# Rows scaled before they are turned, and the last adaptation product moved behind the norm

## The reference, cut to what matters

```
x = x + 0.5 * swiglu(rms_norm(x, ffn1_norm[l]), gate, up, down)      # ffn1, 2816 wide
p = rms_norm(x, mix_norm[l]) @ w_in[l]                                # mixer: latent attention
x = x + concat(attn(p), conv(p)) @ w_out[l]                           #   and a 31-tap convolution
x = x + 0.5 * swiglu(rms_norm(x, ffn2_norm[l]), gate, up, down)      # ffn2
x = rms_norm(x, post_norm[l])
```

```
shift, scale, gate = split(silu(c) @ w_ada[l] + b_ada[l], 3)
h = rms(x, norm_w[l]) * (1 + scale) + shift
```

## Time and profile before

| | |
|---|---|
| median of 3 runs | 2732.62 us (2731.36 to 2739.61) |
| profiled execution, its own time | 2733.47 us |
| its span, first to last instruction | 2731.8 us |
| PE busy | 2438.5 us, 89% |
| PE weight loads busy | 2051.2 us, 75% |
| DVE busy | 1842.4 us, 67% |
| ACT busy | 1150.6 us, 42% |
| mean granted clock of PE | 0.938 |
| DMA moved | 298.41 MB, mean 109 GB/s |
| DMA of constants, latent weights, x | 1904, 2304 and 1024 KB |

### The profile page before, as it was taken

One profiled execution on the slowest core, in us unless ns is written; L12 is line 12 of the kernel. 1 busy time (PEld: TensorE's weight loads), 2 busy tenths in 40 slices (PEclk: granted clock), 3 DMA queues, 4 the chain that ended last, 5 costly groups with the idle time before them and its releaser, 6 DMA issues.

```text
span 2731.8 us, 38970 instructions
## 1 busy us (share of the span) xinstructions
PE 2438.5 (89%) x13968; PEld 2051.2 (75%) x13968; DVE 1842.4 (67%) x3484; ACT 1150.6 (42%) x1747; POOL 89.6 (3%) x140
## 2 busy tenths in 40 slices
PE   7998768997998868997999989999777899999978
PEld 6997458997997448996777777677456788888868
DVE  6775867787775776785455534456334699998884
ACT  4344334434344333334555513323223455555553
POOL 0000000000000000001122101001000000000000
PEclk9999969999999969998999989999888999999998
DMA  6554006555553005554344411111012222222212
GB/s 258 215 192 153 17 8 234 206 189 186 211 203 139 31 8 201 215 192 85 79 71 75 77 39 62 62 46 61 23 61 70 70 77 77 84 84 77 77 58 96
DMA packets 81319, 298.41 MB, mean 109 GB/s; under 512 B 9824, under 2 KB 10336, under 8 KB 80480
## 3 DMA queue, kind: packets, MB, share of 16 engines
q1 hardware_dynamic: 77760, 284.20, 29.4%
q0 software_dynamic: 2048, 4.20, 2.7%
q10 hardware_dynamic: 1440, 9.08, 0.9%
HBM read 296.39 MB, written 1.05 MB: 109 GB/s over the span
## 4 chain that ended last, share of the span: by engine, by line
PE 66%; DVE 24%; ACT 6%; issue 2%; DMA 1%; POOL 0%; DVEq 0%; SPq 0%; ACTq 0%; another core or an unknown queue 0%; POOLq 0%
PE ps L668 45%; PE ps L709 9%; DVE work L1900 3%; DVE wsplit L1761 3%; PE ps L1079 2%; DVE work L1816 1%; DVE work L2378 1%; DVE work L2348 1%; DVE work L2340 1%; PE ps L695 1%; DVE work L2399 1%; ACT wsplit L1241 1%; ACT work L1707 1%; PE ps L951 1%; PE ps L965 1%
## 5 line engine op out<-in xcount | busy, mean ns | idle before, releaser
L668 PE MATMUL ps<-hsplit,wsplit 128*128 128x256 f32 (+1 forms) x9072 | 1503.5, 325 | 32.5 <-DVE hsplit L2037 13.0
L668 PEld LDWEIGHTS ps<-hsplit,wsplit 128*128 128x128 f32 x9072 | 1313.0, 192 | 178.9 <-issue 22.9
L1241 ACT ACTIVATE wsplit<-ring 128x1024 fp32r<-128x1024 f32 x490 | 516.9, 1058 | 708.6 <-PE ps L668 499.0
L1761 DVE TENSOR_TENSOR wsplit<-ring,wsplit 128x1024 fp32r<-128x1024 f32 x490 | 600.8, 1230 | 299.0 <-ACT wsplit L1241 285.5
L709 PE MATMUL ps<-wsplit,fsplit 128*128 128x512 f32 x1056 | 261.5, 397 | 13.6 <-DVE wsplit L1761 8.7
L709 PEld LDWEIGHTS ps<-wsplit,fsplit 128*128 128x128 f32 x1056 | 195.1, 191 | 51.9 <-DVE wsplit L1761 9.6
L1816 DVE SCALAR_TENSOR_TENSOR work<-ring,cs,work 128x128 f32<-128x128 f32 x672 | 206.0, 348 | 9.0
L1316 ACT ACTIVATE work<-ps 128x256 f32<-128x256 f32 x88 | 33.7, 383 | 153.4 <-PE ps L668 153.4
L1900 DVE SCALAR_TENSOR_TENSOR work<-work,vec 128x256 f32<-128x256 f32 x240 | 97.6, 476 | 0.0
L1186 PE MATMUL ps<-work 128*128 128x128 f32 x512 | 71.1, 290 | 24.3 <-DVE work L2399 24.0
L1794 DVE TENSOR_TENSOR work<-ps,work 128x256 f32<-128x256 f32 x88 | 37.3, 424 | 77.0 <-ACT work L1316 76.6
(11 more groups left out here) (312 smaller groups left out, 2545.1 us busy)
## 6 DMA issues: line engine op xcount, KB each, us to landing
ring<-panels SPq DMA_DIRECT2D x538, 512.0 KB, 4.2
work<-latent_weights ACTq DMA_DIRECT2D x2, 2304.0 KB, 12.8
work<-rpb POOLq DMA_DIRECT2D x64, 64.0 KB, 6.7
cst<-constants ACTq DMA_DIRECT2D x1, 1904.0 KB, 9.6
work<-x SPq DMA_DIRECT2D x1, 1024.0 KB, 10.8
work<-post_rows ACTq DMA_DIRECT2D x2, 512.0 KB, 3.9
cT<-ctx ACTq DMA_DIRECT2D x1, 1024.0 KB, 6.6
out<-xT SPq DMA_DIRECT2D x1, 1024.0 KB, 3.9
```

The lines of the kernel that those rows point to most:

```text
L668: ins = mm(out_, w(a), x(b), start=start and n == 0, stop=stop and n == 2, **kw)
L1241: af(wsplit[:, split_slot(name, n), 0, :], ring[:, p % slots, :], ACT.Copy).then_inc(high_ready, 1)
L1761: tt(parts[:, 1, :], ring[:, p % slots, :], parts[:, 0, :].bitcast(fp32), ALU.subtract)\
```

## The change

- The identity scaled by the factors is gone. The rows are scaled instead, into `xs` (the place of `mix`): row tile 0 by DVE, row tile 1 by ACT (`scaled`), each in two instructions of 128 x 512. PE then turns the pieces with sixteen transposes, in the order half 0 of row tile 0, half 0 of row tile 1, and the same for half 1.
- `turned` reads a PSUM bank only when PE is through with it (`bank_full`). The turned tiles lie in seven banks, not eight, and bank 6 is left to the adaptation's sums.
- The twelfth adaptation product of each ffn section goes from the section's end to the next norm: tiles 0 to 5 between DVE's scaling and its `turned`, tiles 6 and 7 behind `turned`. PE's sum goes behind `turn`; the bias is added by `ada_out` behind that.
- In `post_factor` the Exp of `n_r1` is done once for both row tiles, behind the scaling.
- ACT issues only the identity's 128 columns of the constants and the two tables at the start, and the other constants and the latent weights behind its first factor and scaling. The sigmoid of the condition goes behind the first `turned`. DVE's `mixer`, PE's, and POOL wait for the rest of the constants.

```diff
-            def turn(q, src, banks):
-
-                for t in range(2):
-                    pe.wait_ge(row_stage, 4 * q + t + 3)
-                    for k in range(KD):
-                        ins = mm(turned_at(banks, k, t * 128, 128),
-                                 src[:, t, k * 128:(k + 1) * 128], diag_r[:, t, :], start=True, stop=True)
-                        if t == 1:
-                            ins.then_inc(t_done, 1)
+            def turn(q, banks):
+
+                for half in range(2):
+                    for t in range(2):
+                        pe.wait_ge(*((row_stage, 4 * q + 3 + half) if t == 0 else (rstd_ready, 3 * q + 2 + half)))
+                        for k in range(4 * half, 4 * half + 4):
+                            ins = nc.tensor.transpose(turned_at(banks, k, t * 128, 128), xs[:, t, k * 128:(k + 1) * 128],
+                                                      cst[:, K_ID:K_ID + 128])
+                            if t == 1:
+                                ins.then_inc(t_done, 1)
...
+            def ada_sum(l, f, n, i=0):
+
+                pe.wait_ge(ada_acc_ready, l * (2 * ADA_PER_FFN) + (i + (f * ADA_PER_FFN + n + 2)))
+                for v in range(2):
+                    last = mm(ps[:, 6, bass.ds(i * 2 + (2 * n + v), 1)], ada_acc[:, v, :], ones[:, 0:1],
+                              start=True, stop=True)
+                last.then_inc(ada_sum_done, 1)
...
                 down(3 * FT - 1, 1, fb + FT)
-                ada_sum(ADA_PER_FFN - 1)
...
-                turn(l * 3, xg, FFN_BANKS)
+                turn(l * 3, FFN_BANKS)
+                if l > 0:
+                    ada_sum(l - 1, 1, ADA_PER_FFN - 1)
                 ffn("ffn1", l, 0, l * 3)
                 pe.wait_ge(x_ready, l * 16 + 4)
-                turn(l * 3 + 1, xN, MIX_BANKS)
+                turn(l * 3 + 1, MIX_BANKS)
+                ada_sum(l, 0, ADA_PER_FFN - 1)
                 mixer(l)
...
-            turn(LAYERS * 3, xg, LAST_BANKS)
+            turn(LAYERS * 3, LAST_BANKS)
+            ada_sum(LAYERS - 1, 1, ADA_PER_FFN - 1)
             norm(0, sq_ctx)
...
+            def scaled(t, src):
+
+                for half in range(2):
+                    c = slice(half * 512, (half + 1) * 512)
+                    af(xs[:, t, c], src[:, t, c], ACT.Copy, scale=n_rr[:, t:t + 1]).then_inc(rstd_ready, 1)
...
-                for t in range(2):
-                    dve.wait_ge(rstd_ready, 2 * q + t + 1)
-                    ts(diag_r[:, t, :], cst[:, K_ID:K_ID + 128], n_rr[:, t:t + 1], None, ALU.mult).then_inc(row_stage, 1)
+                dve.wait_ge(rstd_ready, 3 * q + 1)
+                for half in range(2):
+                    c = slice(half * 512, (half + 1) * 512)
+                    ts(xs[:, 0, c], src[:, 0, c], n_rr[:, 0:1], None, ALU.mult).then_inc(row_stage, 1)
...
-                ada_products(SLOTS * (FT // 2) - 1, ADA_PER_FFN - 1)
...
                 V.restart()
-                row_factors(l * 3 + 1, 16 * l + 4, 2, 1)
+                row_factors(l * 3 + 1, 16 * l + 4, 2, 1, xN)
+                ada_last(l, 0, range(0, 6))
                 turned(l * 3 + 1, vec[:, V_MIX:V_MIX + 8], MIX_BANKS, "win", l)
+                ada_last(l, 0, range(6, KD))
+                ada_out(l, 0)
                 mixer(l)
...
-            act.dma_start(cst[:, :], consts_in).then_inc(const_loaded, 16)
+            act.dma_start(cst[:, 0:128], consts_in[:, 0:128]).then_inc(const_loaded, 16)
             act.dma_start(vec2[:, :], vec2_in).then_inc(const_loaded, 16)
             act.dma_start(vec[:, :].unsqueeze(1), vecs_in[0:1].rearrange("a p m -> p a m")).then_inc(const_loaded, 16)
-            act.dma_start(lat[:, :].unsqueeze(1), lat_in[0:1].rearrange("a p m -> p a m")).then_inc(lat_loaded, 16)
...
-            act.wait_ge(ada_in, 1)
-            sigmoid(cs[:, 0, :], cs[:, 0, :]).then_inc(ada_sig, 1)
             act.wait_ge(rows_loaded, 16)
             for b in range(4):
                 square(b, xg, 0).then_inc(sq_ready, 1)
-            factor(0)
+            factor(0, xg)
+            act.dma_start(cst[:, 128:NCONST], consts_in[:, 128:NCONST]).then_inc(const_loaded, 16)
+            act.dma_start(lat[:, :].unsqueeze(1), lat_in[0:1].rearrange("a p m -> p a m")).then_inc(lat_loaded, 16)
```

More of the change, by code:

```diff
@@ L341, in build @@
         a_qn = take(1)
-        gw = take(KD, 16)
+        gw = work[:, 20200:20328].rearrange("p (k g) -> p k g", k=KD)
         a_sq = sqf[:, 0:1024].rearrange("p (a t) -> p a t", a=2)
@@ L741, in ffn @@
                 down(4, 0, fb + 1, first=True)
-                ada_sum(0)
+                pe.wait_ge(ada_ready, 2 * l + f)
+                ada_sum(l, f, 0)
                 with pe.Fori(0, FT // 2 - 1) as i:
@@ L894, in _ @@
             pe.wait_ge(h_ready, H_FIRST + 8)
+            pe.wait_ge(ada_ready, 2 * LAYERS)
             for k in range(KD):
@@ L1270, in factor @@
                     A.need()
-                    af(n_rr[:, t:t + 1], n_l1[:, t:t + 1], ACT.Exp, scale=-0.5).then_inc(rstd_ready, 1)
+                    ins = af(n_rr[:, t:t + 1], n_l1[:, t:t + 1], ACT.Exp, scale=-0.5)
+                    if t == 0:
+                        ins.then_inc(rstd_ready, 1)
+                    else:
+                        A.did(ins)
+                        A.need()
+                scaled(1, src)
             def post_factor(q):
@@ L1281, in post_factor @@
                     A.did(af(n_h1[:, c], n_l1[:, c], ACT.Copy, scale=-0.5))
-                    A.did(af(n_r1[:, c], n_l1[:, c], ACT.Exp, scale=-0.5))
                     A.need()
@@ L1787, in normed, with ada_products @@
                     ts(xN[:, t, :], xg[:, t, :], n_r1[:, t:t + 1], None, ALU.mult).then_inc(x_normed, 1)
+            def ada_products(name, l, f, p, n, i=0, tiles=range(KD)):
+                w = ring[:, p % SLOTS, :].rearrange("p (k c) -> p k c", k=KD)
+                done = l * (2 * ADA_PER_FFN) + (i + (f * ADA_PER_FFN + n + 1))
+                if 0 in tiles:
+                    dve.wait_ge(loaded[p % SLOTS], loads_of(name, l, p, i))
+                    dve.wait_ge(ada_sum_done, done)
+                for k in tiles:
+                    for v in range(2):
+                        factor = cs[:, 1, 2 * k + v:2 * k + v + 1]
+                        if k == 0:
+                            ins = ts(ada_acc[:, v, :], w[:, k, :], factor, None, ALU.mult)
+                        else:
+                            if v == 0:
+                                V.need()
+                            ins = stt(ada_acc[:, v, :], w[:, k, :], factor, ada_acc[:, v, :], ALU.mult, ALU.add)
+                        if k == KD - 1 and v == 1:
+                            ins.then_inc(ada_acc_ready, 1)
+                        else:
+                            V.did(ins)
             def ffn(name, l, f):
@@ L2007, in _ @@
                 turned(l * 3, vec[:, V_FFN1:V_FFN1 + 8], FFN_BANKS, "ffn1", l)
+                if l == 0:
+                    dve.wait_ge(ada_sig, 1)
+                    V.did(tt(cs[:, 1, :], cs[:, 0, :], vec2[:, W_C:W_C + 16], ALU.mult))
+                    V.restart()
+                else:
+                    ada_last(l - 1, 1, range(6, KD))
+                    ada_out(l - 1, 1)
                 normed(l)
@@ L2052, in _ @@
             low("A", 0, 0)
+            ada_last(LAYERS - 1, 1, range(6, KD))
+            ada_out(LAYERS - 1, 1)
+            dve.wait_ge(ada_ready, 2 * LAYERS)
+            modulation(1)
             normed(LAYERS)
```

117 lines of the change are left out of this document (58 added, 59 removed).

## The result

The changed kernel took 2744.27 us (median of 6 runs, 2741.32 to 2745.81), the kernel before 2732.56 on the same chip: the ratio is 1.0037, with a 95% interval of 1.0024 to 1.005. By the medians it is 11.7 us slower; by the ratio, which takes in all runs, about 10 (6.6 to 13.7). The forecast of 2742.5 is 1.8 us short. The profiled execution took 2744.67, of which the span is 2743.0; the span before was 2731.8.

What follows compares the result with a forecast made beforehand. Mostly PE bounds the kernel: delays to its next matmul are paid in full. Terms -7.2 + 5.1 + 5.4 + 5.6 + 3.6 - 2 x 1.3 = +9.9 on 2733.47 give 2743.4, as median 2742.5 us; range 2733 to 2749.

Steps and rivals of the forecast that it cites:

- The four stops: Both ffn1 to mixer, ffn2 to ffn1, last ffn2 to A: `ada_sum` waits for DVE's product; 3.8, 4.1, 4.3, 3.6 us lost.
- The cost ahead of the sum: DVE's scaling, product tiles, `turned` and split panel ahead of `ada_sum`, from 225.7 to 235.9; low-clock transposes 0.22 us each.
- Costed at nothing: SP loads slot 6 late (236 instead of 221) with all panels behind it; used 17 us later, so no loss.
- Mixer to ffn2: Both layers, no product there: first matmul earlier by 1.4 us less 0.1 of clock, 1.3 us gained each.
- The opening: Kernel start: loading x and vector tables first brings the first matmul forward; 7.2 us gained, between 4.5 and 8.7.
- Hidden; some 2 us if not: Opening: the delayed 4.2 MB share queues with panels until about 32, yet PE reaches the eighth panel load in time.
- Rival D: Opening: loading first does little, as panels land at their old rate; gains only 2.5 us, total 2747.2; chance 0.06.
- The clock behind the stops: After both ffn1 to mixer and ffn2 to ffn1: PE idles, then restarts at low clock; 1.3 us lost each.
- Rival A: Transposes do not raise PE's clock: opening loses 1.2 us more, each mixer to ffn2 1.3; total 2746.3; chance 0.16.
- Rival B: Stops cost less: opening gains 8.7 us, low clock costs 0.5 instead of 1.3 at three restarts; 2738.6; chance 0.22.
- Rival C: PE's late starts are made up inside the sections; losses of 19.7 us vanish, total 2722.8; chance 0.08.

Runs made afterwards that it cites:

- e1: Changed kernel with only PE's `ada_sum` of the last product moved behind the next section's first two panels (behind the norm before section A): 2720.03 us.
- e4: Changed kernel with the 4.2 MB of constants and latent weights issued behind the first silu instead of the first factor: 2741.13 us.
- e9: Changed kernel with 36 extra identity transposes on PE between turn and sum, at both mixers and between the layers: 2743.53 us.
- e2: Changed kernel with the last product, its sum and its bias back at the end of the ffn section, ahead of the norm: 2720.23 us.
- e6: e2 with the turn's sixteen one-pass transposes written as two-pass matmuls against the identity: 2732.75 us.
- e10: Changed kernel with sums and their read later, constants behind the first silu, and 24 identity transposes ahead of each turn behind an ffn: 2717.97 us.

## Why the prediction was right, and where it was off

**The four stops: right, mechanism and size.** The forecast put 15.8 us on `ada_sum` standing between the turn and the section; the profile shows 15.4, each with the bracket that names VectorE's product at L1843. e1 shows the cause: with only those sums moved the kernel is 24 us faster. That is more than 15.4 and the clock's 5.2, because the sum also hid what the change gains at the same places: from the last down product of the first ffn1 (209.23) to the mixer's first product (223.68) it is 14.45 us in e1, 20.16 in the changed kernel and 16.36 before.

**The cost ahead of the sum: right.** VectorE's scaling (0.44 a piece where 0.4 was taken), tiles, split and panel took the 10.0 us from 221.98 to 231.95 where 10.2 were forecast, and a transpose at the low clock takes 3.65/16 = 0.23 where 0.22 was taken, in a range of 0.12 to 0.30. "Costed at nothing" was right too: the load of slot 6 came late, and e1 lost nothing by it.

**Mixer to ffn2: right in size** (1.3 and 1.8 gained against 1.4), but its clock was costed at 0.1 and took 1.0 of the first: the transposes are over 3.7 us after they began, the clock had not risen by then, and the products behind them ran at half of it until about 429. At the second it rose at the end of the transposes and cost nothing.

**The opening: the term that was mis-sized.** "Hidden; some 2 us if not", said of the 4.2 MB put back behind the first factor. They were not hidden, and they cost more than 2: -8.5 to the first product, +0.15 in the 96 products, +1.8 more of waiting at the first down (4.00 against 2.20), +2.7 from there to the next group, nearly all because the wait had halved the clock (5.49 against 3.06). That gives -3.9 for -7.2. The step looked at the eighth load and not at the loads already under way: the chain's transfer of 18.95 us, which ends as ScalarE takes the first down's panel at 28.47, began at 9.41, ahead of the two. e4 takes 3.0 us back at this place (33.81 for 36.80). Rival D, which said that panels would hold the opening back, was right in that; the gain lies between its 2.5 and the forecast's 7.2.

**The clock behind the stops: right mechanism, mis-sized.** 2.3, 1.4 and 1.5 for 1.3 each: in the earlier trace rows the low stretch was taken as 3.0 us, and in the changed kernel the clock was 0.50 from 232 to about 238. In e9 the filled wait gave the full 2.3 back at the first place. The forecast had the turn raise the clock and the wait lose it again; at the first place the turn did not raise it at all. Against this stand some 3.5 us less inside the sections, which the forecast held at nothing; that is why an error of 3.3 us in the opening and 2.2 more of lost clock (1.3 and 0.9) left only 1.8 us of error in the end. The 3.5 us are no loss made up: 3.1 of them are the two first down products at which the clock fell in one execution and not in the other, as it did at half of such products in all. That the forecast came out within 2 us is in this part luck.

**Rival A fell, but not in every place**: transposes can raise the clock, as the windows from 639 to 642 show, 0.50 to 1.00 with nothing else on TensorE since 637.15. They did so within three of the six turns, and the first mixer to ffn2, with its 1.0 us, went as A said (1.3). The Trainium skill, "TensorE: Matmul & The Clock Gate", Part 4 (PE-mode transpose), has it that transposes do not count as TensorE being busy; these rows do not agree. In e9, too, only transposes ran from 222.69 to 231.08, and the clock rose among them, at 227.9, and held at 1.00 up to the products, where in the changed kernel it was 0.50.

**Rival B** asked for cheaper stops; they cost their price and their clock more. **Rival C** (made up in the section) fell: of the 18 us from which it decides, at most the 3.5 came, and 3.1 of these are the two clocks above.

**What stays open.** e2 and e1 are equal though e1 relieves the time ahead of the adds; e1's first product stands 1.2 us further behind the first transpose (4.44 against 3.27), waiting for the split, and VectorE is late at the first down between the layers (4.21 us), which accounts for much of it, but the sum was not closed. The part from section A to the end took between 1451.7 and 1457.3 us in the single executions profiled, whatever the kernel; why was not tried. And what decides whether the clock falls behind a wait of 2.18 us is not shown.

## What to carry to other kernels

When work is moved behind a critical step on one engine, move its reader on every in-order engine too: the reader belongs behind the point at which the work ends by the profile, not behind the step it was moved past. A queue of transfers that is "hidden" has to be compared with each panel's own landing time, not with the time the last of them is needed. Cost a wait on TensorE twice, as time and as the clock of the products after it. And before a difference of a few us between two single traces is explained, look in both for the short stretches in which the clock fell: here two of them, in places that the change did not touch, were 3.1 us.

## What the runs showed of the hardware

- Sixteen 128x128 fp32 transposes took 3.65 us at granted clock 0.50 (0.23 each) and 36 took 4.95 us with the clock rising within them (e9); the same turn as 32 matmul passes took 5.37, with the clock rising at 226.3 within them (e6).
- The clock did not follow at once what TensorE did. It stayed at 1.00 for some 3 us without any work (641.3 to 644.3, above); in e10 it fell under running transposes, behind an idle time of 3.82 us, and in e9's second mixer under running products, behind one of 1.68, where the same filling had held it at the first.
- With about 418 GB/s moving on all the queues from 9.4 to 28.4 us, one 512 KB panel needed 18.95 us, where the median panel lands in 4.2. With the 4.2 MB issued later (e4) the same panel needed 7.5.
- Behind the same wait of 2.18 or 2.19 us on TensorE, the twelve products of a first down took about 3.04 us at 16 places and 4.4 to 4.6 at 15, with the granted clock 0.50 in them.
- In several kernels with the same opening the first 96 products took 11.9 us or 13.2 to 13.7, by when the clock rose. In e1 TensorE ran 6 or 7 products in each us from 15 to 18 and 10 or 11 from 18 on, in the changed kernel 9 or 10 from 15 on. The clock column says 1.00 all along in both; its record begins only at 18.1 in e1 and at 12.9 in the changed kernel, so it cannot be read ahead of that. That spread of 1.5 us for one stretch is as large as most effects looked for here.
